# Scattering expert rows to slots by token and rank, and adding them on VectorE, instead of adding them in DRAM

## What is computed

```python
u = rms_norm(h, norm_ffn[layer]) * (1 + sc2) + sh2
h = h + g2 * grouped_moe(u, w_router, b_router, w_gate[layer], w_up[layer], w_down[layer])
# grouped_moe: 16 experts in 4 groups. For each token one group is chosen, in it the top 2
# experts; gates is zero for the 14 others
for e in range(N_EXPERTS):
    hid = jax.nn.silu(t @ w_gate[e]) * (t @ w_up[e])
    out = out + gates[:, e:e + 1] * (hid @ w_down[e])
```

## Time and profile before

| | |
|---|---|
| median of 3 runs | 756.32 us (754.42 to 756.67) |
| the profiled execution, its own time | 755.94 us |
| span of the profile | 753.9 us |
| mean granted TensorE clock | 0.945 of full speed |
| busy: PE / VectorE / ScalarE / GpSimd | 670.7 / 339.3 / 180.3 / 98.8 us |
| HBM read, written | 193.06 MB, 27.30 MB |

### The profile page before, as it was taken

How to read it: one execution, slowest core, us unless ns; L and a number is a source line. 1 busy time by engine, 2 the same in 40 slices (tenths; PEclk the granted TensorE clock), 3 DMA queues, 4 the chain that set the end, 5 groups by cost and what they waited for, 6 DMA issues and landing times. The chain is left out here.

```text
span 753.9 us, 7442 instructions
## 1 busy us (share of the span) xinstructions
PE 670.7 (89%) x2565; PEld 353.8 (47%) x2565; DVE 339.3 (45%) x631; ACT 180.3 (24%) x454; POOL 98.8 (13%) x84
## 2 busy tenths in 40 slices
PE   4999999998999939999999999299599999999960
PEld 3455444444444725545545544198354554554520
DVE  3135798989943355323223222246642322322312
ACT  5002232333324212212212211136211221221212
POOL 0010000000000320121221220200202122122020
PEclk9999999999999858999999999799599999999995
DMA  9999989887864295488988971499508799898316
GB/s 342 382 334 397 354 280 351 311 286 266 314 252 168 82 380 209 171 324 295 338 322 303 346 246 27 110 423 376 215 1 323 291 336 336 312 338 315 122 24 239
DMA packets 55877, 204.32 MB, mean 271 GB/s; under 512 B 9530, under 2 KB 18806, under 8 KB 43556
## 3 DMA queue, kind: packets, MB, share of 16 engines
q1 hardware_dynamic: 45012, 183.62, 63.6%
q0 software_dynamic: 10256, 19.53, 10.8%
q10 hardware_dynamic: 576, 0.74, 0.3%
HBM read 193.06 MB, written 27.30 MB: 292 GB/s over the span
## 5 line engine op out<-in xcount | busy, mean ns | idle before, releaser
L1588 PE MATMUL ps<-ring,work 128*128 128x512 f32 x384 | 169.8, 595 | 0.0
L1588 PEld LDWEIGHTS ps<-ring,work 128*128 128x128 f32 x384 | 73.0, 191 | 90.9 <-issue 90.2
L860 DVE SCALAR_TENSOR_TENSOR acc<-adaw,cond,acc 128x1024 f32<-128x1024 f32 x70 | 89.9, 1284 | 10.5 <-DMA adaw<-in_w_ada_dram 8.4
L546 POOL DMA_INDIRECT h_dram<-work x32 | 51.3, 1602 | 307.2 <-DVE work L1188 272.8
L1165 DVE TENSOR_TENSOR work<-work,ps 128x256 f32<-128x256 f32 x32 | 13.5, 422 | 168.6 <-ACT work L769 168.5
L1613 PE MATMUL psY<-ring,work 128*128 128x512 f32 x192 | 86.6, 593 | 1.2 <-ACT work L779 1.2
L1428 PE MATMUL psY<-xu,ring 128*128 128x512 f32 x192 | 85.6, 598 | 0.0
L1188 DVE SCALAR_TENSOR_TENSOR work<-psY,work,gbc 128x512 f32<-128x512 f32 x64 | 45.1, 747 | 74.2 <-PE psY L1613 74.2
L769 ACT ACTIVATE work<-ps 128x256 f32<-128x256 f32 x32 | 12.3, 383 | 272.3 <-PE ps L1588 272.3
L1428 PEld LDWEIGHTS psY<-xu,ring 128*128 128x128 f32 x192 | 35.5, 190 | 46.1 <-issue 45.9
L1588 PE MATMUL ps<-xu,work 128*128 128x512 f32 x128 | 56.2, 592 | 0.0
(11 more groups left out here) (192 smaller groups left out, 649.7 us busy)
## 6 DMA issues: line engine op xcount, KB each, us to landing
adaw<-in_w_ada_dram SPq DMA_DIRECT2D x84, 512.0 KB, 5.5
ring<-in_w_gate_dram SPq DMA_DIRECT2D x24, 1024.0 KB, 5.7
ring<-in_w_up_dram SPq DMA_DIRECT2D x24, 1024.0 KB, 8.2
ring<-in_w_down_dram SPq DMA_DIRECT2D x24, 1024.0 KB, 12.4
xu<-in_w_gate_dram SPq DMA_DIRECT2D x8, 1024.0 KB, 5.2
xu<-in_w_up_dram SPq DMA_DIRECT2D x8, 1024.0 KB, 7.6
xu<-in_w_down_dram SPq DMA_DIRECT2D x8, 1024.0 KB, 12.0
work<-in_w_ada_dram SPq DMA_DIRECT2D x12, 512.0 KB, 9.2
```

The lines of the kernel that those rows point to most:

```text
L546: pool.indirect_dma_start(out=h_dram[l], out_offset=bass.IndirectOffsetOnAxis(tok_i[:, e:e + 1], 0), in_=yrow[:, e % 2, :], in_offset=None ...
L860: dve.scalar_tensor_tensor(total, adaw[:, n % ABUF, :], cond[:, k:k + 1], total if k else brow[:, :], ALU.mult, ALU.add).then_inc(mac_step, 1)
L1588: ins = pe.matmul(gu_ps[j % 2][:, :].rearrange("p (a f) -> p a f", a=2), xgT[:, j % 2, k, :], w_gu(j % 4)[:, :, k, :], start=(k == 0), sto ...
```

## The change

The DRAM buffer `h_dram[l]` of 512 rows becomes `y_dram[l]` of 1024 rows: row 2 x token + rank takes what the token's expert of that rank (0 or 1) gives. `h` isn't stored any more and stays in SBUF. The scatter is a plain write, and no scatter waits for another. A sixth column of the table carries the rank, and `targets` computes the row `dst_i`. At the end of a layer SP loads both rows of each token, 1 MB per tile, into two free areas (`y_back`), and VectorE adds them to `h` one after the other (`add_back`) before ScalarE may norm the tile.

```diff
-TC, TOKC = 5, 2
+TC, TOKC = 6, 2
+GC = TC - TOKC
...
+        y_back = [xg[:, 0:2], xg[:, 2:4], *(xu[:, (T + i) * D:(T + i + 2) * D].rearrange("p (r d) -> p r d", r=2)
+                                            for i in (0, 2))]
...
 for t in range(T):
     sp.wait_ge(xhat_ready, (2 * l + 1) * T + t + 1)
-    sp.dma_start(h_dram[l][t * P:(t + 1) * P, :], h[:, t, :]).then_inc(h_stored, 16)
     sp.dma_start(xhat_dram[l][t * P:(t + 1) * P, :], xhat[:, t, :]).then_inc(xhat_stored, 16)
...
 for t in range(T):
-    sp.dma_start(h[:, t, :], h_dram[l][t * P:(t + 1) * P, :]).then_inc(h_back[t], 16)
+    sp.dma_start(y_back[t], y_dram[l][2 * t * P:2 * (t + 1) * P, :].rearrange("(p r) d -> p r d", r=2)
+                 ).then_inc(y_back_in[t], 16)
...
 def scatter(e):
     pool.wait_ge(y_ready, HEAD + l * E + e + 1)
-    if e > E // 2 + 1:
-        pool.wait_ge(y_out[e % 2], 16 * (l * E // 2 + (e - 2) // 2 + 1))
-    elif e:
-        pool.wait_ge(y_out[(e - 1) % 2], 16 * (l * E // 2 + (e - 1) // 2 + 1))
-    else:
-        pool.wait_ge(h_stored, 16 * T * (l + 1))
     pool.indirect_dma_start(
-        out=h_dram[l], out_offset=bass.IndirectOffsetOnAxis(tok_i[:, e:e + 1], 0),
-        in_=yrow[:, e % 2, :], in_offset=None, bounds_check=SEQ - 1, oob_is_err=False,
-        compute_op=ALU.add).then_inc(y_out[e % 2], 16)
+        out=y_dram[l], out_offset=bass.IndirectOffsetOnAxis(dst_i[:, e:e + 1], 0),
+        in_=yrow[:, e % 2, :], in_offset=None, bounds_check=2 * SEQ - 1, oob_is_err=False
+        ).then_inc(y_out[e % 2], 16)
...
 # ScalarE, norm(s, t)
-    act.wait_ge(h_back[t], 16 * (s // 2))
+    act.wait_ge(h_summed, (s // 2 - 1) * T + t + 1)
...
+def add_back(l, t):
+    dve.wait_ge(y_back_in[t], 16 * (l + 1))
+    link(dve.tensor_tensor(h[:, t, :], h[:, t, :], y_back[t][:, 0], ALU.add))
+    dve.tensor_tensor(h[:, t, :], h[:, t, :], y_back[t][:, 1], ALU.add).then_inc(h_summed, 1)
...
 # VectorE, route(l), between the gate's bf16 parts
+    dve.tensor_copy(rtab[:, :, :, 5], rank.rearrange("p (t e) -> p t e", t=T))
...
+def targets(half):
+    n = E // 2
+    cols = slice(half * n, half * n + n)
+    t3 = tab[:, 0:n * GC].rearrange("p (e c) -> p e c", c=GC)
+    link(dve.scalar_tensor_tensor(dst_i[:, cols], tok_i[:, cols], 2.0, t3[:, :, 3], ALU.mult, ALU.add))
...
 gates(l, 1)
 tokens(l, 3)
+targets(1)
...
 gates(l, 0)
 tokens(l, 2)
+targets(0)
...
 # VectorE, start of layer 1
-    for t in range(T):
-        norm(2, t)
+    add_back(0, 0)
+    for t in range(1, T):
+        add_back(0, t)
+        norm(2, t - 1)
+    norm(2, T - 1)
...
 # VectorE, end of the kernel: norm_out(t) is the reciprocal and L1277
+add_back(1, 0)
+for t in range(1, T):
+    add_back(1, t)
+    norm_out(t - 1)
+norm_out(T - 1)
...
 # TensorE, start of layer 1
-    pe.wait_ge(h_back[0], 16)
+    pe.wait_ge(y_back_in[0], 16)
     keep_clock(1)
```

More of the change, by code:

```diff
@@ L69, in trunk @@
 def trunk(nc, x, c, w_ada, b_ada, norm_mix, norm_ffn, w_in, w_out, sinks, conv_w, w_pool, pool_scale,
-          w_router, b_router, w_gate, w_up, w_down, norm_final, consts, pool_mats, out, mod_dram, xhat_dram, h_dram):
+          w_router, b_router, w_gate, w_up, w_down, norm_final, consts, pool_mats, out, mod_dram, xhat_dram, y_dram):
     ctx = ExitStack()
@@ L150, in trunk @@
         hT = take(2 * P).rearrange("p (a s) -> p a s", a=2)
-        tok_i = take(E).bitcast(U32)
+        tok_i, dst_i = take(E).bitcast(U32), take(E).bitcast(U32)
         gslot = take(E)
@@ L154, in trunk @@
         rtab = take(T * E * TC // 2).bitcast(BF16).rearrange("p (t e c) -> p t e c", t=T, e=E)
-        tab = take(2 * EPG * TC)
+        tab = take(E // 2 * TC)
         ovtab = take(8)
-        ovtok = take(1).bitcast(U32)
+        ovtok, ovdst = take(1).bitcast(U32), take(1).bitcast(U32)
         ovgate = take(1)
@@ L269, in trunk @@
         y_out = [sem(f"y_out{j}") for j in range(2)]
-        h_stored = sem("h_stored")
-        h_back = [sem(f"h_back{t}") for t in range(T)]
+        y_back_in = [sem(f"y_back_in{t}") for t in range(T)]
+        h_summed = sem("h_summed")
         nfin_in = sem("nfin_in")
@@ L581, in _ @@
                         pool.wait_ge(ov_y[l], n + 1)
-                        pool.reg_add(bound, zero, SEQ - 1)
+                        pool.reg_add(bound, zero, 2 * SEQ - 1)
                         pool.indirect_dma_start(
-                            out=h_dram[l], out_offset=bass.IndirectOffsetOnAxis(ovtok[:, 0:1], 0),
-                            in_=yrow[:, 0, :], in_offset=None, bounds_check=bound, oob_is_err=False,
-                            compute_op=ALU.add).then_inc(ov_out[l], 16)
+                            out=y_dram[l], out_offset=bass.IndirectOffsetOnAxis(ovdst[:, 0:1], 0),
+                            in_=yrow[:, 0, :], in_offset=None, bounds_check=bound, oob_is_err=False
+                            ).then_inc(ov_out[l], 16)
         @block.scalar
@@ L1136, in tokens @@
                 at0 = PLACE_OF[TABLE[i][0]]
-                t3 = tab[:, 0:n * TOKC].rearrange("p (e c) -> p e c", c=TOKC)
+                part = tab[:, GC * E // 2:GC * E // 2 + n * TOKC]
+                t3 = part.rearrange("p (e c) -> p e c", c=TOKC)
                 dve.wait_ge(table_banked, l * TABLES + i + 1)
-                link(dve.tensor_copy(tab[:, 0:n * TOKC], table_ps[i][:, at0 * TOKC:(at0 + n) * TOKC]))
+                link(dve.tensor_copy(part, table_ps[i][:, at0 * TOKC:(at0 + n) * TOKC]))
                 dve.scalar_tensor_tensor(tok_i[:, at0:at0 + n], t3[:, :, 0], FAR, t3[:, :, 1], ALU.add, ALU.add
@@ L1147, in gates @@
                 cols = slice(half * n, half * n + n)
-                t3 = tab[:, 0:n * 3].rearrange("p (e c) -> p e c", c=3)
+                t3 = tab[:, 0:n * GC].rearrange("p (e c) -> p e c", c=GC)
                 dve.wait_ge(table_banked, l * TABLES + half + 3)
-                link(dve.tensor_copy(tab[:, 0:n * 3], ps5[:, 64 + half * 3 * n:64 + (half + 1) * 3 * n]))
+                link(dve.tensor_copy(tab[:, 0:n * GC], ps5[:, 64 + half * GC * n:64 + (half + 1) * GC * n]))
                 link(dve.tensor_tensor(gslot[:, cols], t3[:, :, 0], t3[:, :, 1], ALU.add))
                 link(dve.tensor_tensor(gslot[:, cols], gslot[:, cols], t3[:, :, 2], ALU.add))
+            def targets(half):
+                n = E // 2
+                cols = slice(half * n, half * n + n)
+                t3 = tab[:, 0:n * GC].rearrange("p (e c) -> p e c", c=GC)
+                link(dve.scalar_tensor_tensor(dst_i[:, cols], tok_i[:, cols], 2.0, t3[:, :, 3], ALU.mult, ALU.add))
             def expert_loop(l):
@@ L1228, in expert_loop @@
                             dve.wait_ge(ov_link[l], HEAD + base + 2)
+                            dve.scalar_tensor_tensor(ovdst, ovtok, 2.0, ovtab[:, 5:6], ALU.mult, ALU.add)
                             dve.tensor_tensor(ovgate, ovgate, ovtab[:, 4:5], ALU.add).then_inc(ov_idx[l], 1)
@@ L1273, in _, with norm_out @@
             dve.wait_ge(nfin_in, 16)
-            for t in range(T):
+            def norm_out(t):
                 dve.wait_ge(std_done, 4 * T + t + 1)
@@ L1561, in gate_table @@
                 for e in sum(TABLE[3:] if half else TABLE[:3], ()):
-                    at0 = 64 + PLACE_OF[e] * 3
+                    at0 = 64 + PLACE_OF[e] * GC
                     for t in range(T):
-                        ins = pe.matmul(ps5[:, at0:at0 + 3], hot(e)[:, t, :], rtab[:, t, e, TOKC:TC],
+                        ins = pe.matmul(ps5[:, at0:at0 + GC], hot(e)[:, t, :], rtab[:, t, e, TOKC:TC],
                                         start=(t == 0), stop=(t == T - 1))
@@ L1748 @@
     args.append([nc.dram_tensor(f"xhat_dram{l}", (SEQ, D), F32, kind="Internal").ap() for l in range(LAYERS)])
-    args.append([nc.dram_tensor(f"h_dram{l}", (SEQ, D), F32, kind="Internal").ap() for l in range(LAYERS)])
+    args.append([nc.dram_tensor(f"y_dram{l}", (2 * SEQ, D), F32, kind="Internal").ap() for l in range(LAYERS)])
     trunk(nc, *args)
```

## The result

The changed kernel takes 769.14 us (767.89 to 770.20), the kernel before 756.50 us in the same runs (754.42 to 759.41): ratio 1.0154, 95% interval 1.0120 to 1.0188. On a second chip the same two stood at 769.75 and 758.80, ratio 1.0122 (1.0089 to 1.0156). The forecast was 771.0 and slower. The profiled execution took 770.08 us for a span of 767.8.

A forecast was written before the change was run, and what follows sets the result against it. TensorE was taken to bound the expert loop, so only layer starts, turn and end counted. 8.6 + 9.3 - 2.8 + 2.0 - 1.2 - 1.3 = +14.6 on 755.94 gave 770.5, as median 771.0 us; range 763 to 778.

The forecast's parts named there:

- Step 1: At both layer ends: 1 MB loads per tile and VectorE's adds cost +8.6 us at the turn, +9.3 at the end.
- The ladder of loads: Read-back at a layer's end: the four tiles land 4.8, 7.3, 9.8 and 12.3 us after SP's first issue.
- Rival (a): At the layer ends the read-back is slower than weight loads and DMA sets the pace: 775 us, chance 0.10.
- Step 2: Last scatter of each layer: a plain one lands sooner, -1.4 us each, -2.8 us in all.
- Step 3: Turn between layers: TensorE's clock is low at the last tile, +2.0 us, bounds 0 and +3.
- Step 4: Start of each layer's experts: without `h` stores first gathers gain, -1.2 us in layer 0, -1.3 in layer 1.
- Step 5: Rank's copy, wider copy, `targets`, four-column gate products and new waits: 0 us in all.
- Rival (c): Layers wait for the adding scatter's tail; 14.8 us at both ends go almost wholly: 756 us or just under, chance 0.04.
- Rival (b): Scatter and store reliefs reach their bounds, the clock at the turn costs nothing: +6.7 us, 763 us, chance 0.15.
- Rival (d): Scatters still pace each other through two `yrow` buffers; Step 2 and Step 4 give nothing: 775 us, chance 0.08.

The follow-up runs named there:

- e2: The changed kernel without VectorE's two adds per tile, both rows still read back: 760.90 us, ratio 1.0032 to the kernel before.
- e1: The kernel before with plain scatters in place of adding ones, all else kept: 752.22 us against 757.43, ratio 0.9915.
- e8: The changed kernel unchanged, run again beside other experiments on one chip: 769.75 us.
- e3: The changed kernel with the eight `h` stores put back, to a buffer no one reads: 770.71 us, ratio 1.0170 to the kernel before.
- e6: The kernel before with the `h` stores moved behind the fourth expert's load and the first gathers: 756.77 us against 758.80, ratio 0.9956.
- e5: The changed kernel with one 128x512 product behind each of three tiles' logits in layer 1: 769.45 us against 769.75 unchanged.
- e7: The kernel before with late `h` stores as in e6 and the three wide products of e5: 756.61 us, ratio 0.9958.

## Why the prediction was right

The direction and the range held: 769.1 lies in 763 to 778, 1.9 below the forecast. That it came so close is in good part luck. The four steps measured +8.3 us between the two profiled executions, not +14.6: the read-back and the adds came out 1.2 us cheaper, the last scatters 3.7, the clock at the turn 1.2 and the stores 0.2. Two things outside the sum filled most of the gap in this pair of profiles, 3.84 us in layer 1's logits and 1.76 ahead of the change.

**Step 1, the read-back and the adds, +17.9: 16.7 measured** (7.95 + 8.73). The ladder of loads is confirmed bare by e2, VectorE sets the pace with its adds, as the forecast had it. It is 1.2 us cheaper because an instruction of VectorE that follows on one of another tile starts some 0.1 us before that one ends in the trace, where the sum counted gaps. Rival (a) is out: no add but the first waits.

**Step 2, the last scatters, -2.8: -6.5.** This is the step that failed. Its bounds, 0 to -3.4 each, held for the end (-2.84) and were passed at the turn (-3.70); the choice within them was wrong. I took the quickest gather, 4.6 us, as the nearest row, and a plain scatter landed in 3.4 and 3.19 us; e1 shows that the add in the DMA alone makes the difference to 7.1 and 6.05. The gather didn't run alone. It was issued at 538.22, the last weights landed at 539.1, other gathers ran beside it, and over 538.2 to 542.8 the DMA share was 0.49. But that doesn't settle why it took longer. The next gather, issued at 539.52 with all weights in and a share of 0.32, took 4.8 us, and a store of 2.6 us ran at a share of 0.69. Whether a gather that has the engines to itself would land in 3.2 us as well, or whether its direction costs more, no run shows. What surroundings can do is plain from the scatters of the changed kernel: 8.3 to 9.3 us while weights stream at a share of 1.0, 2.8 to 3.6 for the last four of each layer. The estimate by the Trainium skill, DMA: Bandwidth & Descriptors, Anatomy of one DMA, 2.6 us for the transfer and -6.9 for the term, was nearer than my row, if 0.6 to 0.8 us short on the transfer. The 4.6 us gather, which I held against it, was no evidence on a scatter at a layer's end.

**Step 3, the clock at the turn, +2.0: +0.83.** The low level at the last tile was right; it rose sooner:

```profile
498.00:500.00 2.00, 1.67 (x7) 1.67 (x8) 1.19 (x3) 0.89 (x3) 0.00 (x0) 0.50 1.04 438
500.00:502.00 2.00, 2.00 (x13) 2.00 (x13) 0.49 (x1) 0.86 (x2) 0.00 (x0) 0.65 0.97 410
502.00:506.00 4.00, 4.00 (x34) 3.97 (x33) 1.55 (x3) 1.30 (x3) 0.00 (x0) 1.00 1.02 424
```

TensorE was at work from 498.3, on tile 2's products, before the last `xhat` at 499.9, and the clock rose within 500 to 502, whose mean is 0.65. I had counted the low stretch from the last tile on. The repeat (e8) has 5.97 us there, +1.09.

**Step 4, the stores that go, -2.5: -3.45 at the gathers, and -2.7 with the pieces around them** (+0.66, +0.47 and -0.34). In layer 0 the mechanism and the size are as forecast, -1.2 net: five of the seven profiles without the stores ahead of the weights show 1.0 to 1.3 us less than the three with them, e3's among these. In layer 1 the 1.01 us at the gather came for a reason that I didn't have, the router that was 3.8 us late. e6 shows the forecast's mechanism there where it isn't late, but its net gain of 0.4 us is within what profiles differ by, so the forecast's -1.3 for layer 1 isn't confirmed.

**Step 5, the small additions, 0: not to be seen.** In the loop of layer 0 0.5 us are more, in that of layer 1 0.3 less.

**What no step had: the logits of layer 1.** +3.84 us in the profiled executions is the largest error. It needn't be a cost of the change as such: e1, with the turn of the kernel before, shows the low stretch too, and the one profile of the kernel before, at clock 0.945, was of the best sort (its executions at that clock took 754.8 to 755.9 us, others up to 764.4). e5 and e7 show that wide products between the logits keep the clock up. Why both profiles of the changed kernel are low there is open. Without this stretch and the 1.76 us ahead of the change, 8.3 of the 13.9 us between the spans are left. The medians say more, 11.0 and 12.6 us, and no run shows that the low stretch explains it. The kernels of e8 and e6 differ by steps 1 to 3 and by `h` stores that come late in the one and not at all in the other, and their medians by 13.0 us; e5 and e7 are the same two with the wide products, both hold the clock up through most or all of the logits, and still lie 12.8 us apart. By the pieces steps 1 to 3 add up to 11.0. So the clock in the logits accounts for the gap between these two profiles, but some 2 us of the medians' difference have no place in the account.

Rival (c) fell short: the ends gave 6.5 us of the 14.8 that it needed. Rival (b), 763, put the four steps at +6.7 and is nearer to their measured +8.3 than the forecast's +14.6. Its -6.9 for the scatters was right to 0.4 us, though its own sign, a landing below 3 us, didn't come for the two that count (3.4 and 3.19). It missed the total by the clock in the logits, as my sum did. Rival (d) is out; by its own terms it stood at 776, not 775.

## What to carry to other kernels

Where a trace has no transfer of the same kind, direction and surroundings, the nearest row is one guess between bounds: here a gather at 4.6 us stood for a scatter that took 3.2 to 3.4. An accumulating scatter costs 2.8 to 3.7 us more than a plain one, and only where someone waits for its landing; paying for that with twice the bytes on the way back and two passes of VectorE over them costs 8 to 9 us per stage. Look first for what the change does by the way: moving the `h` stores out from ahead of the weights and gathers, and nothing else, gave 756.8 against 758.8 us, where the change lost 11. And compare terms as well as totals, for a total can be right by errors that cancel.

## What the runs showed of the hardware

An adding indirect DMA with 128 row indices, on average 64 of them in bounds, of 4 KB each, keeps POOL 1.54 to 2.47 us, and the last one of a layer lands 7.1 and 6.05 us from its start; a plain one keeps POOL 0.96 to 1.19 us, and the last one lands in 3.4 and 3.19. While weights stream at a DMA share of 1.0 plain ones take 8.3 to 9.3 us. The clock can fall to 1.2 GHz while TensorE is busy without a gap: in the changed kernel it was at work all through 522 to 530, with products of 16 columns and transposes, and the clock went from 1.00 to 0.50 within 524 to 526. With a 128x512 product behind each of three tiles' logits it stayed at 1.00 to 534 in e5 and to the end of the logits in e7. The Trainium skill, TensorE: Matmul & The Clock Gate, Part 1, ties the clock to activity and warns of idle gaps; these rows show a fall with no gap in them. Executions of the kernel before, 23 on one chip, differed by 9.6 us, in step with their mean clock.
